# Weight pieces 528 bytes apart in a one-core, three-layer transformer kernel on Trainium2

## The reference

```python
proj = h @ w_in                       # nsa, swa and hybrid mixers
a = jax.nn.relu(h @ w_up); y = (a * a) @ w_down          # width 4096, two layers
q = (h @ wq); kv = mem_n @ wkv; out = o @ wo             # cross-attention
u = h @ w_up                          # 2 * 2816 columns
out = (jax.nn.silu(gate) * val) @ w_down
```

## Time and profile before

| what | value |
|---|---|
| median of three runs | 2047.81 us (2042.06 to 2047.92) |
| span of the profiled execution, first to last instruction | 2041.0 us |
| TensorE matmuls: busy, count | 1973.7 us (97%), 10293 |
| TensorE weight loads: busy, count | 1617.8 us (79%), 10293 |
| VectorE busy | 1131.7 us (55%) |
| GpSimd busy | 945.6 us (46%) |
| ScalarE busy | 701.7 us (34%) |
| mean granted TensorE clock | 0.991 |
| DMA | 252.22 MB, mean 124 GB/s |

### The profile page before, as it was taken

How to read it: one execution, slowest core, us unless ns; L and a number is a source line. 1 busy time by engine, 2 the same in 40 slices (tenths; PEclk the granted TensorE clock), 3 DMA queues, 4 the chain that set the end, 5 groups by cost and what they waited for, 6 DMA issues and landing times.

```text
span 2041.0 us, 27018 instructions
## 1 busy us (share of the span) xinstructions
PE 1973.7 (97%) x10293; PEld 1617.8 (79%) x10293; DVE 1131.7 (55%) x1747; ACT 701.7 (34%) x1225; POOL 945.6 (46%) x552
## 2 busy tenths in 40 slices
PE   6998999999999999999999999999999999999997
PEld 5888777778888887877888888788797788888885
DVE  7675775973545567766322314686453368345163
ACT  3353654432222233654222213342443342222222
POOL 1465553465444445554544444542373244444442
PEclk9998999999999999999999999999999999999998
DMA  7765331545555524721332233221342223333331
GB/s 290 240 216 165 113 102 48 200 163 188 195 176 196 170 68 130 207 88 52 114 98 99 93 96 101 63 83 63 103 145 83 71 70 118 93 93 99 97 93 62
DMA packets 79989, 252.22 MB, mean 124 GB/s; under 512 B 12160, under 2 KB 12672, under 8 KB 79616
## 3 DMA queue, kind: packets, MB, share of 16 engines
q1 hardware_dynamic: 79872, 250.61, 38.0%
HBM read 235.21 MB, written 15.37 MB: 123 GB/s over the span
## 4 chain that ended last, share of the span: by engine, by line
PE 73%; issue 12%; POOL 7%; DVE 5%; ACT 3%; POOLq 0%; DVEq 0%; ACTq 0%
PE ps L909 20%; PE ps L911 20%; PE ps L910 20%; POOL wl L802 6%; PE ps L1195 2%; PE ps L1135 2%; ACT pr L2687 2%; PE ps L1167 1%; PE ps L1472 1%; DVE st L1947 1%; PE ps L1497 1%; POOL al L858 1%; PE ps L977 1%; POOL x L850 1%; PE ps L957 0%
## 5 line engine op out<-in xcount | busy, mean ns | idle before, releaser
L802 POOL TENSOR_TENSOR wl<-raw,wh 128x1024 fp32r<-128x1024 f32 x309 | 770.9, 2501 | 946.9 <-ACT wh L2540 946.7
L2540 ACT CAST wh<-raw 128x1024 fp32r<-128x1024 f32 x309 | 322.3, 1050 | 905.7 <-PE ps L911 840.5
L909 PE MATMUL ps<-ah,wh 128*128 128x512 f32 x904 | 357.7, 396 | 1.5 <-DVE pair L1877 1.5
L910 PE MATMUL ps<-ah,wl 128*128 128x512 f32 x904 | 352.8, 390 | 0.0
L911 PE MATMUL ps<-al,wh 128*128 128x512 f32 x904 | 352.6, 390 | 0.0
L909 PE MATMUL ps<-hh,wh 128*128 128x512 f32 x688 | 270.7, 393 | 1.9 <-DVE hl L2488 1.7
L911 PE MATMUL ps<-hl,wh 128*128 128x512 f32 x688 | 270.3, 393 | 0.0
L910 PE MATMUL ps<-hh,wl 128*128 128x512 f32 x688 | 268.0, 390 | 0.0
L909 PEld LDWEIGHTS ps<-ah,wh 128*128 128x128 f32 x904 | 170.1, 188 | 40.2 <-issue 2.6
L910 PEld LDWEIGHTS ps<-ah,wl 128*128 128x128 f32 x904 | 170.2, 188 | 36.3 <-issue 1.5
L911 PEld LDWEIGHTS ps<-al,wh 128*128 128x128 f32 x904 | 170.1, 188 | 36.0
(11 more groups left out here) (402 smaller groups left out, 3262.7 us busy)
## 6 DMA issues: line engine op xcount, KB each, us to landing
raw<-in_units SPq DMA_DIRECT2D x309, 512.0 KB, 3.5
ada_mlp<-in_ada SPq DMA_DIRECT2D x64, 512.0 KB, 3.6
ada<-in_ada SPq DMA_DIRECT2D x16, 512.0 KB, 15.7
qs<-qscr SPq DMA_DIRECT2D x32, 256.0 KB, 3.4
ada_in<-in_ada SPq DMA_DIRECT2D x16, 512.0 KB, 3.6
ks<-kscr SPq DMA_DIRECT2D x24, 256.0 KB, 4.4
x<-in_xT SPq DMA_DIRECT2D x1, 2048.0 KB, 13.5
qscr<-rot_h SPq DMA_DIRECT2D x16, 128.0 KB, 2.4
```

Source lines behind the costliest of these rows:

```text
L802: nc.gpsimd.tensor_tensor(wl[:, slot], raw[:, slot], wh[:, slot].bitcast(F32), ALU.subtract).then_inc(lo_done, 1)
L909: nc.tensor.matmul(out_ap, wh[:, slot, k], high[:, k0 + k], start=first and k == 0, stop=False)
L910: nc.tensor.matmul(out_ap, wl[:, slot, k], high[:, k0 + k], start=False, stop=False)
L2540: a.copy(wh[:, slot], raw[:, slot]).then_inc(hi_done, 1)
```

## The change

The pieces of `wh` and `wl` are placed 132 numbers (528 bytes) apart in place of 128 (512 bytes): each tile is allocated with rows of 132 and used through a view of its first 128 columns. A slot then takes 4224 bytes in place of 4096, and each of the two tiles 16.5 KiB. Tiles from 112 KiB to the table move up by 1 KiB. To make room, the tile for the rounded masks is dropped: `prev` and `diag` are swapped in the table so that they lie in the order that the products want, and DVE rounds them where they are. `w0` and everything above it stay where they were: 1 KiB more below, 1 KiB less for the masks. `raw`, `ah`, `al`, `x` and `y` stay too. ACT's rounding and POOL's subtraction now write (and POOL reads, for wh) eight runs of 128 numbers with gaps, and no longer one run of 1024. No instruction is added, removed or moved.

```diff
+ROW = P + 4
+PAD = 1
...
-SMALL = (("ones", P), ("ident", P), ("diag", P), ("prev", P), ("cmp_add", SC * P),
+SMALL = (("ones", P), ("ident", P), ("prev", P), ("diag", P), ("cmp_add", SC * P),
...
-    wh = at("wh", 80, [P, RING, DC, P], F32R)
-    wl = at("wl", 96, [P, RING, DC, P], F32R)
-    rs = at("rs", 112, [P, 2, S])
-    tt = at("tt", 116, [P, 3, S])
-    sq = at("sq", 122, [P, 2, S])
-    sm = at("sm", 126, [P, SMALL_COLS])
-    s1 = 126 + (SMALL_COLS * 4 + 63) // 64 / 16
+    wh = at("wh", 80, [P, RING, DC, ROW], F32R)[:, :, :, 0:P]
+    wl = at("wl", 80 + RING * DC * ROW / 256, [P, RING, DC, ROW], F32R)[:, :, :, 0:P]
+    rs = at("rs", 112 + PAD, [P, 2, S])
+    tt = at("tt", 116 + PAD, [P, 3, S])
+    sq = at("sq", 122 + PAD, [P, 2, S])
+    sm = at("sm", 126 + PAD, [P, SMALL_COLS])
+    s1 = 126 + PAD + (SMALL_COLS * 4 + 63) // 64 / 16
...
-    mask_r = at("mask_r", k1 + 1.5, [P, 2, P], F32R)
-    w0 = k1 + 2.5
+    mask_r = at("mask_r", 126 + PAD + COL["prev"][0] / 256, [P, 2, P], F32R)
+    w0 = k1 + 1.5
```

More of the change, by code:

```diff
@@ L315, in build @@
     pair = at("pair", w0, [P, 4, S])
-    acc_in = at("acc_in", 112, [P, 1024])
+    acc_in = at("acc_in", 112 + PAD, [P, 1024])
     rot_h = at("rot_h", w0 + 12, [P, 2, 2, S], F32R)
@@ L321, in build @@
     vtmp = at("vtmp", w0 + 36, [P, 2, S])
-    ada_in2 = at("ada_in2", 116, [P, 2, 1024])
+    ada_in2 = at("ada_in2", 116 + PAD, [P, 2, 1024])
     xb_h = [at(f"xb_h{i}", (w0 + 44, 48)[i], [P, 16, 4 * NCMP], F32R) for i in range(2)]
     xb_l = [at(f"xb_l{i}", (w0 + 52, w0 + 36)[i], [P, 16, 4 * NCMP], F32R) for i in range(2)]
-    hp = at("hp", 124, [P, 2, 2 * P])
+    hp = at("hp", 124 + PAD, [P, 2, 2 * P])
     gate_t = at("gate_t", 56, [P, S])
@@ L339, in build @@
     pos_i = at("pos_i", 60, [P, S], I32)
-    trig = at("trig", 112, [P, 2, S])
+    trig = at("trig", 112 + PAD, [P, 2, S])
     qs = at("qs", w0 + 16, [P, 4, S], F32R)
```

## The result

The changed kernel takes 2067.08 us (median of 4 runs, 2065.81 to 2069.48) against 2045.47 us of the kernel before: a ratio of 1.0108, with a 95% interval of 1.0094 to 1.0123, about 22 us more. The forecast was 2029 us; the time lies above the top of the range, 2066, and rival B had the sign. Profiled spans went from 2041.0 to 2065.7 us, 24.7 more.

A forecast was written before the change was run, and what follows sets the result against it. TensorE, busy 97% of the span, was taken to bound the kernel through the distance between matmul starts. Terms of -5.4, -12.6, -1.6 and +0.4 gave -19.2 us, from 2047.8 to 2028.6, say 2029 us; range 2000 to 2066 us.

The forecast's parts named there:

- rival B: Weight position changing with each k keeps TensorE's stream unsettled at 232.2 ns: 28 us more, 2076 us; chance 0.23.
- What bounds the kernel: TensorE, busy 97% of the span; the cost of a matmul is the distance between starts, 226.7 to 233.3 ns at 512 columns.
- ACT, POOL, masks and moved tiles at 0: Gapped writes on ACT and POOL, masks rounded in place, tiles moved 1 KiB: 0 us; bound for the writes 2 us more.
- Pieces 528 bytes apart: Weight pieces of TensorE's products: surplus falls from 13.3 to 11.7 ns as in compress, so 225.0 ns at 512 columns.
- the term for ah: 3168 products with ah and al moving, from 226.7 to 225.0 ns each: 5.4 us less.
- the one for hh, fh and oh: 3240 products with hh, fh and oh moving, from 228.9 to 225.0 ns each: 12.6 us less.
- It should not matter much whether the moving row is on the grid or half way: 512-column products on TensorE: 225.0 ns is an average over eight positions, for moving rows at either start.
- half the price: Half of the slowdown forecast under rival B, about 2060 us; much of its 0.23 chance went here.
- the nine distances after other work: Start of an ah stream before steady values, 529.51 to 531.60 us: 232.2 ns each, taken as the unsettled price.
- xoh: 192 products with xoh moving, from 233.3 to 225.0 ns each: 1.6 us less.
- 256 columns: Products with 256 moving columns, either weights or mh and ml moving: together 0.4 us more.
- Rival A: TensorE's two operands hardly meet any more, distances fall towards 216 ns: 82 us less, 1966 us; chance 0.12.

The follow-up runs named there:

- the undo run: Changed kernel with pieces 512 bytes apart again, masks still rounded in place and tiles still moved: 2043.47 us against 2044.90 us for the kernel before, ratio 0.9993.
- TensorE alone: Separate program, other engines silent: kernel's product triples with moving rows offset m bytes and weights s; 226.7 ns at m = 0, s = 0; 232.0 with step 528.
- the two programs: Two separate programs running only TensorE; the second added offsets, swapped roles and offsets alternating by k: 232.2 ns for 0 and 16 in turn.

## Why the prediction was wrong

- *What bounds the kernel*: right. The product stream, and in it the distance between starts, carried the effect; the granted clock, the waits and the times of ACT's and POOL's steps did not move.
- *ACT, POOL, masks and moved tiles at 0*: right, by the undo run and by the groups above.
- *Pieces 528 bytes apart, "As the surplus on the grid does not depend on the number of columns, I carry 11.7 over to 512 columns: 225.0 ns"*: **this is the step that failed.** The surplus over one column a cycle is indeed 13.3 ns at 256, 384 and 512 columns when both operands are on the grid (120.0, 173.3, 226.7). With a step of 528 it is not the same: 10.8 ns at 256, 15.6 at 384 (175.6 - 160.0) and 18.7 at 512. In the text's own terms the term for ah is +17.1 us by the steady values and +16.1 by the products one by one, and not -5.4; the one for hh, fh and oh is +10.4 or +9.6, and not -12.6. A rule read from two rows with the operands in the same place was used for eight other places. These have another price at 512 columns (231.6 on average when fixed) than at 256 (118.2), and the best place at 256 columns, 64 bytes off, is one of the slow ones at 512.
- *"It should not matter much whether the moving row is on the grid or half way"*: right, 232.1 and 232.0 ns.
- *Rival B*: right in sign, and near in the price of a product (232.2 against 232.1 measured; the total of 2076 us was 9 too high, the 2060 for "half the price" was 7 too low). Its mechanism did not come true: the stream settles into a pattern that repeats. By the estimate from the fixed values, some three quarters of the loss is what the eight places cost even when they stay, which B did not have, and the rest comes from changing place. That the nine distances after other work have nearly the mean of the changed kernel may be chance; no run ties the two together. B was given 0.23 because of "compress changes position just as often and does not rise; but it has 256 columns". The caveat held the answer: the trace had no row with this step at 512 columns, and the one with 256 was carried over.
- *xoh*: its 233.3 was read as a stream that "never comes down". It is a steady pattern of three distances, and TensorE alone gives the same 233.3 with ah at m = 64 and al at m = 0. With the moving rows on one grid it fell to 226.7; with the stagger its uninterrupted triples average 231.3, and the term is 0.4 us less in place of 1.6.
- *256 columns*: forecast 0.4 us more in all; in the two traces no class of these products moved by more than 0.7 us.
- *Rival A*: the distance of about 216 ns that the Trainium skill has for 512 columns ("TensorE: Matmul & The Clock Gate", "Back-to-back issue gap"), which that section calls the gap of a single matmul, was reached at no place tried, and still less its figure of about 131 ns for a stream of loads and matmuls: 226.7 is the least in all settings of 512 columns with a weight load for each product. Its rule in "SBUF — State Buffer" ("Who interferes with whom"), that TensorE never waits on anyone, agrees with these runs as far as other engines go (the same distances with them silent). It has nothing on the places of TensorE's own two operands, and these move a product from 226.7 to 236.7 ns.

## What to carry to other kernels

In a stream of float32r products of 512 columns that loads weights each time, let the weight piece and the moving row start at the same place modulo 256 bytes, for every product of the stream. This gave 226.7 ns at the five places 0, 32, 64, 128 and 192, but not at 16. Check it by the distance between starts, which no busy share shows. Don't pad rows by one step as a reflex: at 512 columns steps of 528, 544, 576 and 640 bytes between pieces all cost 4.7 to 5.3 ns a product, and one of 768 nothing. A surplus measured at one number of columns must not be carried to another unless rows at both show the operands in the same two places. And a distance above the best one is no sign of disorder: print single distances and look for the period before calling a stream unsettled.

## What was not expected of the hardware

- Sixteen bytes in the place of an operand move a 512-column product by 6.7 ns (226.7 against 233.3, offsets 16 and 32), and a step of 640 bytes between pieces costs while one of 768 does not.
- The best distance depends on the number of columns: 0 for 512 (226.7 against 233.3 at 64), 64 or 192 for 256 (113.3 against 120.0 at 0).
- The same products at the same places have two steady rates, 226.7 and 232.2 ns, in the run with `wl` 16 bytes off, and which one holds depends on how the stream began. One setting gave different values in the two programs (moving rows and weights both 16 bytes off: 230.0 and 231.1), so other values between 228 and 237 may also hang on what ran before them; each setting was run once, in one order.
- What in TensorE or SBUF makes the patterns is not shown. No model of banks or ports was tested on the chip, and none is claimed.
